# Adding the pooling branch into the merged tile by accumulating DMAs from GpSimd's queue, instead of loading it and adding it on VectorE

## The chip, the cores and the metric

The kernel runs on one core of a Trainium2 chip. The metric is the device time of one execution in microseconds (us): 1882.92 us, the median of three runs (1879.91 to 1883.15).

## What is computed

The reference is one hybrid decoder layer over 512 positions and a model width of 2048, in float32. Cut to the part that the change touches:

```python
merged = sigmoid(gate_pool) * (y_pool @ w_pool_out) + sigmoid(gate_dn) * (y_dn @ w_dn_out)
h = h + merged @ w_o
return rmsnorm(h[:, N_META:], final_norm_w)
```

`y_pool` is 1024 wide, `y_dn` 2048 wide, and `w_dn_out` and `w_o` are 2048 x 2048. Ahead of this come a combined input projection, a pooling mixer and a chunked gated DeltaNet, in which nothing is changed.

## The kernel before

**Layout.** Activations lie transposed: a tile is 128 output channels (partitions) by 512 positions. `merged` has 16 such tiles, k = 0 to 15. Every float32 product is made of three fp32r products: a matrix is split in a high part (a ScalarE copy, `wh`, `xh`, `mh`) and a low part (a VectorE subtraction, `wl`, `xl`, `ml`).

**Stages.** (1) Input projection and both mixers. (2) The pool units: 16 units n, each `y_pool @ w_pool_out` for 128 channels, times its gate (`g0a`, `g0b`, `g0c`), stored by GpSimd's queue in the DRAM scratch `pool_d` (`unit_stored` counts the landings). (3) Eight output blocks for `y_dn @ w_dn_out`, b = DN0 to END - 1, called j = 0 to 7 below; block j makes the tiles `merged[2j]` (c = 0) and `merged[2j+1]` (c = 1). (4) The product with `w_o`: four column blocks, each over the 16 tiles k in order, then residual, norm and store.

**An output block.** It is a Strassen-like product of 2 x 2 quarters with seven products (order 7, 6, 2, 5, 4, 3, NEXT; the last one belongs to the next block, and block 7 has six). Each product is two chunks of 12 matmuls, so a block has 14 chunks, t = 0 to 13 (12 in block 7). Every engine has its own program for a block, written as a loop over t:

- SyncE (`block_loads`) loads the four quarters of the next block's weights into `raw`, 512 KB each. The first load waits for the sum S4 (line 1913) of the block that runs, the second, right behind it, for the eighth low part of a split; the others for later splits. The second load brings the quarter of the product NEXT.
- ScalarE (`block_acts`) makes the high parts (line 1324) some four chunks ahead, snapshots of accumulators, and `last_to_time`, a copy of one accumulator to half of `merged[2j]`.
- VectorE (`block_steps`) makes the low parts (line 1883), the sums of quarters S3, S2, S1, S4 (lines 1891, 1899, 1905, 1913) that the weights of later products need, and the results c22, c21, c11 (lines 1927, 1920, 1934).
- TensorE waits for each chunk for its low part (`lo_done`), then for what the product needs.

The hook `branch(t)` puts the work of the merge into these loops. Before, ScalarE makes `last_to_time` at t = 12 of block j. VectorE multiplies `merged[2j+1]` by its gate `g1` at t = 10, and `merged[2j]` at t = 13 (`weighed_by_gate`, line 2499; each counts up `mg_step`). At t = 5 of the blocks 2 to 5 VectorE adds one tile of the pooling branch (`m_whole`, line 2510), ScalarE makes the high part (`m_split`), and VectorE the low part (`m_low`, line 2515). The tiles 4 to 15 go through the same three steps in the first column block of stage 4, each beside a split of `w_o` (`split_c`, lines 1324 and 2504).

**Where the pooling branch comes from.** SyncE loads `pool_d` back in four pieces of 1 MB (`load_gated`, line 894): the first ahead of block 0's loads, two when the last chunk of block 7 is done, the fourth after the tile multiplications. The gates `g1` are loaded from ScalarE's queue: those of blocks 0 and 1 (`second_gates`, line 1828) behind the last split before block 0 and ahead of block 0's first snapshot, those of block j + 1 at t = 10 of block j, 256 KB x 2 each.

Of the kernel before, what the change touches and what calls it, by code (L numbers as in the profile page):

```python
# [7 lines left out]
ALU = mybir.AluOpType  # L8
# [3 lines left out]
P = 128  # L12
D = 2048
SEQ = 512
# [5 lines left out]
KT = D // P  # L20
# [28 lines left out]
CW = 256  # L49
# [110 lines left out]
def base_of(b):  # L160

    return counted(b, "chunk")
# [76 lines left out]
def build(nc, x, meta_tokens, norm_w, w_in, conv_w, A_log, dt_bias, pool_mix, pool_scale, dn_norm_w,  # L239
# [10 lines left out]
    with outer:  # L250
# [5 lines left out]
        def sem(name):  # L256
            return outer.enter_context(nc.semaphore(name))
# [43 lines left out]
        def layout(number):  # L301
            made = Layout()
            made.stack_id = number
            return made
# [125 lines left out]
        def set_at(product_of):  # L430

            return X_AT + 2 * XA * XPLACE.index(product_of)


        lay = layout(8)
        lay.skip_to(KT * SEQ)
        gated_last = lay.tensor("gated_last", [4, SEQ])
        gated_first = lay.tensor("gated_first", [4, SEQ])
        lay.skip_to(set_at(3))
        gated_set = lay.tensor("gated_set", [2, 4, SEQ])  # L440
        lay.close()
        gated = [gated_first[:, :, :], gated_set[:, 0, :, :], gated_set[:, 1, :, :], gated_last[:, :, :]]


        lay = layout(7)
        xsum = {}
        for product_of in XPLACE:
# [86 lines left out]
        unit_done, unit_stored = sem("unit_done"), sem("unit_stored")  # L534
        yd_loaded = [sem("yd_loaded0"), sem("yd_loaded1")]
        g1_loaded = [sem("g1_loaded0"), sem("g1_loaded1")]
        mg_step, mg_done = sem("mg_step"), sem("mg_done")
        gated_loaded = [sem("gated_loaded0"), sem("gated_loaded1")]

        m_hi, m_lo = sem("m_hi"), sem("m_lo")  # L540
        w_hi, w_lo, w_used, c_done, res_done = sem("w_hi"), sem("w_lo"), sem("w_used"), sem("c_done"), sem("res_done")
# [121 lines left out]

            return (n + 2) % 3

        def m_step(j, t):


            return j - 2 if t == 5 and 2 <= j < 6 else None

        def c0_of(kind):

# [83 lines left out]
        def _(sp):  # L756
# [128 lines left out]
            for units, pieces in ((NUNIT - 2, ((RA, 11), (buffer_of(DN0, DN0 % 2, 7), 21))),  # L885
                                  (NUNIT, ((RF, 22), (buffer_of(DN0, DN0 % 2, 2), 12)))):
                sp.wait_ge(w_lo, 2 * units)
                for slot, quarter in pieces:
                    load_raw(slot, quarter, 0, w_dn_out)

            def load_gated(i):

                rows = pool_d[4 * P * i:4 * P * (i + 1), :].rearrange("(k p) t -> p k t", p=P)
                sp.dma_start(gated[i], rows).then_inc(gated_loaded[i % 2], 16)

            sp.wait_ge(x_lo, SET_LO + 4 * len(SET_SPLITS))
            sp.wait_ge(unit_stored, 16 * NUNIT)
            load_gated(0)
            for b in range(DN0, END - 1):
                block_loads(b, b % 2, (b + 1 - DN0) * CW, None, w_dn_out)  # L900

# [11 lines left out]
            for u in range(4):  # L913
                load_c(u)
            sp.wait_ge(pe_chunk, base_of(END))
            for i in range(1, 3):
                load_gated(i)
            x_rows = x[0].rearrange("(n p) d -> p n d", p=P)
            for i in range(2):
                sp.dma_start(res[:, :, i * 1024:(i + 1) * 1024], x_rows[:, :, i * 1024:(i + 1) * 1024]).then_inc(res_loaded, 16)  # L920
            sp.wait_ge(add_done, counted(END, "add"))
            sp.dma_start(fnw[:, :], final_norm_w.unsqueeze(0).broadcast_to([P, D])).then_inc(fnw_loaded, 16)
            sp.wait_ge(mg_step, KT)
            sp.wait_ge(mg_done, 8)
            load_gated(3)
            for u in range(4, 4 * NCB):
                load_c(u)
            for n in range(4):
# [393 lines left out]
        def _(act):  # L1322
# [71 lines left out]
            def last_to_time(b, par, kind, dst):  # L1394

                act.wait_ge(pe_chunk, last_added(b))
                for part, cols in placed(kind, not eight(b), dst):
                    ins = copy(part, bank_a[par][:, cols])
                ins.then_inc(last_done, 1)
# [415 lines left out]

            def m_split(k):

                act.wait_ge(mg_done, k + 1)
                copy(mhs[k], merged[:, k, :]).then_inc(m_hi, 1)

            def second_gates(j):

                if j > 1:
                    act.wait_ge(mg_step, 2 * j - 2)
                else:
                    act.wait_ge(x_lo, SET_LO + 3 * len(SET_SPLITS))
                for c in range(2):
                    act.dma_start(g1[:, j % 2, c, :], gates_d[D + j * CW + c * P:D + j * CW + (c + 1) * P, :]).then_inc(g1_loaded[j % 2], 16)

            for j in range(2):  # L1830
                second_gates(j)
            for b in range(DN0, END):
                def branch(t, b=b):
                    j = b - DN0
                    if t == 12:
                        last_to_time(b, b % 2, "gate", merged[:, 2 * j, :])
                    if t == 10 and 0 < j < END - 1 - DN0:
                        second_gates(j + 1)
                    if m_step(j, t) is not None:
                        m_split(m_step(j, t))  # L1840
                    if b == END - 1 and t in C_SPLITS:
                        split_c(0, C_SPLITS.index(t))
                block_acts(b, b % 2, "gate", "gate", branch, no_hook)

            last_to_time(END - 1, (END - 1) % 2, "gate", merged[:, KT - 2, :])

            def squares(blk, n):
# [25 lines left out]
        def _(dve):  # L1873
# [629 lines left out]
                dve.wait_ge(w_hi, C_SPLIT + KT * blk + kt + 1)  # L2503
                tt(cwl[kt], rawc[kt // 4][:, kt % 4, :], cwh[kt].bitcast(F32), ALU.subtract).then_inc(w_lo, 1)  # L2504

            def m_whole(k):

                dve.wait_ge(gated_loaded[k // 4 % 2], 16 * (k // 8) + 16)
                dve.wait_ge(mg_step, 2 * (k // 2) + (1 if k % 2 == 1 else 2))
                tt(merged[:, k, :], merged[:, k, :], gated[k // 4][:, k % 4, :], ALU.add).then_inc(mg_done, 1)  # L2510

            def m_low(k):

                dve.wait_ge(m_hi, k + 1)
                tt(ml[:, k, :], merged[:, k, :], mhs[k].bitcast(F32), ALU.subtract).then_inc(m_lo, 1)
# [4 lines left out]
            for b in range(DN0, END):  # L2520
                def branch(t, b=b):
                    j = b - DN0
                    if t == 13:
                        weighed_by_gate(j, 0)
                    if t == 10:
                        weighed_by_gate(j, 1)
                    if m_step(j, t) is not None:
                        m_whole(m_step(j, t))
                        m_low(m_step(j, t))
                    if b == END - 1 and t in C_SPLITS:  # L2530
                        split_c(0, C_SPLITS.index(t))
                block_steps(b, b % 2, "gate", [merged[:, 2 * (b - DN0) + c, :] for c in range(2)], no_wait, branch, no_hook)

            weighed_by_gate(END - 1 - DN0, 0)

            def residual(blk, n):
# [14 lines left out]

            for kt in range(4, KT):
                split_c(0, kt)
                m_whole(kt)
                m_low(kt)
            for blk in range(1, NCB):
                for kt in range(KT):
# [21 lines left out]
        def _(pool):  # L2579
# [89 lines left out]
            def gate_load(n):  # L2669

                pool.dma_start(g0[unit_gate(n)], gates_d[n * P:(n + 1) * P, :]).then_inc(g0_loaded[unit_gate(n)], 16)

            pool.wait_ge(pe_chunk, ALL_CHUNKS)
            pool.wait_ge(add_done, counted(NCP, "add"))
            for c in range(2):
# [3 lines left out]
            for n in range(NUNIT):  # L2679
                pool.wait_ge(unit_done, n + 1)  # L2680
                pool.dma_start(pool_d[n * P:(n + 1) * P, :], g0[unit_gate(n)]).then_inc(unit_stored, 16)
                pool.wait_ge(unit_stored, 16 * n + 16)
                if n + 3 < NUNIT:
                    gate_load(n + 3)
# [1 line left out]
_INS = ["x", "meta_tokens", "norm_w", "w_in", "conv_w", "A_log", "dt_bias", "pool_mix", "pool_scale", "dn_norm_w",  # L2686
        "w_pool_out", "w_dn_out", "w_o", "final_norm_w"]
# [14 lines left out]
```

## Time and profile before

| | |
|---|---|
| median of 3 runs | 1882.92 us |
| the profiled execution, its own time | 1879.91 us |
| its span in the profile | 1877.8 us |
| TensorE matmul busy | 1828.2 us, 97% |
| VectorE, ScalarE, GpSimd busy | 73%, 55%, 6% |
| stage 3, from the first chunk of block 0 | 1536.4 to 1695.8 us |
| stage 4, matmuls | 1695.8 to 1870.0 us |
| mean granted clock of TensorE | 0.996 of full speed |

A timeline row has start, duration, engine, line, operation, output and inputs, and in square brackets the idle time of the engine ahead of it with what ended it. A row with "x2" merges two instructions in a row. DVE is VectorE, ACT ScalarE, PE TensorE, POOL GpSimd, SP SyncE; a "q" behind the name is the engine's sequencer. In the profile's DMA rows q0 is the queue that GpSimd feeds, q1 SyncE's, q10 ScalarE's.

### The profile page before, as it was taken

What the parts mean: (1) busy time and instruction counts of PE and PEld (TensorE: products, weight loads), DVE (VectorE), ACT (ScalarE), POOL (GpSimd) and SP (SyncE); (2) the same over time, 40 slices, a digit from 0 to 9 for tenths busy, and PEclk for the clock granted to TensorE, in tenths of its full rate; (3) what the DMA queues carried; (4) which work ended last, traced back from release to release, by engine and by line L of the source; (5) the groups of instructions that cost most, each with busy time, mean ns of one, the idle gap of its engine ahead of it and who ended that gap; (6) DMA issues with size and microseconds to landing.
All of it is one profiled execution on the core that took longest, in us unless ns stands there. A gap on an engine that the chain in (4) does not pass through costs nothing.

```text
span 1877.8 us, 39178 instructions
## 1 busy us (share of the span) xinstructions
PE 1828.2 (97%) x15889; PEld 1746.1 (93%) x15889; DVE 1378.1 (73%) x2440; ACT 1029.7 (55%) x2299; POOL 120.1 (6%) x156
## 2 busy tenths in 40 slices
PE   7999999999999999999999999999999999999998
PEld 6999999999999999999999998999999889998886
DVE  7777878778787887868788687777785857886442
ACT  6445456566575756757566574645554434444331
POOL 1100000101010010101001010000000110000000
PEclk9999999999999999999999999999999999999999
DMA  6342455555275554536555265455645755467402
GB/s 197 106 127 66 119 163 151 130 148 159 86 199 140 160 130 141 153 110 183 137 146 157 86 189 139 115 167 146 157 119 178 231 184 150 117 190 286 151 23 90
DMA packets 332133, 273.51 MB, mean 146 GB/s; under 512 B 12841, under 2 KB 283650, under 8 KB 331298
## 3 DMA queue, kind: packets, MB, share of 16 engines
q1 hardware_dynamic: 302528, 201.43, 37.9%
q0 software_dynamic: 12992, 39.57, 7.7%
q10 hardware_dynamic: 16434, 30.00, 4.5%
q8 instruction: 126, 2.06, 0.5%
q14 instruction: 53, 0.43, 0.1%
HBM read 225.22 MB, written 46.79 MB: 145 GB/s over the span
## 4 chain that ended last, share of the span: by engine, by line
PE 71%; DMA 9%; DVE 9%; ACT 6%; issue 4%; POOL 1%; ACTq 0%; DVEq 0%; SPq 0%; POOLq 0%
PE pj L1012 43%; PE pj L971 10%; PE pg L939 10%; PE pj L939 5%; PE pt L939 3%; ACT wh L1324 2%; DVE wl L1883 2%; DMA dec<-in_consts 1%; DMA pool_out_scratch<-g0a 1%; DMA pool_out_scratch<-g0b 1%; DVE raw L1913 1%; DMA pool_out_scratch<-g0c 1%; DMA dec<-gate_sum_scratch 1%; PE pt L1144 1%; DVE stg L2227 1%
## 5 line engine op out<-in xcount | busy, mean ns | idle before, releaser
L1012 PE MATMUL pj<-xh,wh 128*128 128x256 f32 (+1 forms) x3016 | 876.4, 291 | 9.4 <-ACT snap L1324 4.5
L1012 PE MATMUL pj<-xl,wh 128*128 128x256 f32 (+1 forms) x3016 | 850.8, 282 | 0.0
L1012 PE MATMUL pj<-xh,wl 128*128 128x256 f32 (+1 forms) x3016 | 850.8, 282 | 0.0
L1324 ACT ACTIVATE wh<-raw 128x512 fp32r<-128x512 f32 x882 | 533.8, 627 | 529.8 <-PE pj L1012 173.3
L1883 DVE TENSOR_TENSOR wl<-raw,wh 128x512 fp32r<-128x512 f32 x854 | 573.8, 689 | 312.4 <-ACT wh L1324 297.3
L1012 PEld LDWEIGHTS pj<-xh,wh 128*128 128x128 f32 x3016 | 569.9, 189 | 19.0 <-ACT snap L1324 6.8
L1012 PEld LDWEIGHTS pj<-xl,wh 128*128 128x128 f32 x3016 | 571.1, 189 | 0.8 <-issue 0.7
L1012 PEld LDWEIGHTS pj<-xh,wl 128*128 128x128 f32 x3016 | 569.8, 189 | 0.0
L971 PE MATMUL pj<-xh,wh 128*128 128x260 f32 (+2 forms) x648 | 185.7, 287 | 3.1 <-DVE wl L1883 3.1
L971 PE MATMUL pj<-xh,wl 128*128 128x260 f32 (+2 forms) x648 | 183.7, 284 | 0.0
L971 PE MATMUL pj<-xl,wh 128*128 128x260 f32 (+2 forms) x648 | 183.4, 283 | 0.0
L971 PEld LDWEIGHTS pj<-xh,wh 128*128 128x128 f32 x648 | 122.7, 189 | 3.6 <-POOL xl L2593 3.4
L971 PEld LDWEIGHTS pj<-xl,wh 128*128 128x128 f32 x648 | 122.9, 190 | 0.2 <-issue 0.2
L971 PEld LDWEIGHTS pj<-xh,wl 128*128 128x128 f32 x648 | 122.5, 189 | 0.0
L2227 DVE SCALAR_TENSOR_TENSOR stg<-xin,convcur,stg 128x528 f32<-128x528 f32 x144 | 109.9, 763 | 8.0 <-ACT stg L1537 7.3
L1324 ACT ACTIVATE snap<-pj 128x256 f32<-128x256 f32 (+2 forms) x182 | 68.7, 378 | 33.4 <-PE pj L1012 21.9
L2504 DVE TENSOR_TENSOR cw_low<-cw_raw,cw_high 128x512 fp32r<-128x512 f32 x64 | 42.6, 689 | 54.6 <-ACT cw_high L1324 54.6
L1899 DVE TENSOR_TENSOR raw<-raw 128x1024 f32<-128x1024 f32 x54 | 66.1, 1224 | 6.3 <-DVE wl L1883 0.5
L1324 ACT ACTIVATE cw_high<-cw_raw 128x512 fp32r<-128x512 f32 x64 | 38.4, 626 | 58.4 <-PE pt L939 29.7
L1905 DVE TENSOR_TENSOR raw<-raw 128x1024 f32<-128x1024 f32 x54 | 65.8, 1219 | 0.0
L1891 DVE TENSOR_TENSOR raw<-raw 128x1024 f32<-128x1024 f32 x54 | 65.8, 1219 | 0.0
L1913 DVE TENSOR_TENSOR raw<-raw 128x1024 f32<-128x1024 f32 x54 | 65.8, 1218 | 0.0
(325 smaller groups left out, 2258.0 us busy)
## 6 DMA issues: line engine op xcount, KB each, us to landing
raw<-in_w_in SPq DMA_DIRECT2D x224, 512.0 KB, 4.7
head_scratch<-stg ACTq DMA_DIRECT2D x64, 264.0 KB, 3.8
raw<-in_w_dn_out SPq DMA_DIRECT2D x32, 512.0 KB, 5.4
cw_raw<-in_w_o SPq DMA_DIRECT2D x16, 1024.0 KB, 6.0
kq<-head_scratch SPq DMA_DIRECT2D x8, 1056.0 KB, 9.7
gates_scratch<-stg ACTq DMA_DIRECT2D x32, 256.0 KB, 2.0
raw<-in_w_pool_out SPq DMA_DIRECT2D x7, 1024.0 KB, 5.9
tm<-head_scratch SPq DMA_DIRECT2D x8, 528.0 KB, 3.6
```

Source lines behind the costliest of these rows:

```text
L939: return pe.matmul(dst, lhs, rhs, start=start, stop=stop)
L971: mm = pe.matmul(banks[bank][:, c0:TH], w[:, slot, k, :], xx[factor][:, kt, c0:TH], start=chunk in opened and one and k == 0, stop=chunk i ...
L1012: mm = pe.matmul(bank[:, c0:TH], w[:, slot, k, :], xx[what][:, kt, c0:TH], start=opens and one and kt == 0, stop=closes and last and kt == ...
L1144: mm = pe.transpose(pt[rows, i * P:(i + 1) * P], src, ident)
L1324: return act.activation(dst, src, ACT.Copy)
L1883: tt(wl[:, slot, :, :], raw[:, buffer_of(of, par, what), HK * half:HK * (half + 1), :], wh[:, slot, :, :].bitcast(F32), ALU.subtract).then ...
L1891: tt(tile, tile, raw[:, RA, :, :], ALU.add).then_inc(sum_done, 1)
L1899: tt(tile, tile, raw[:, RF, :, :], ALU.add).then_inc(sum_done, 1)
L1905: tt(raw[:, buffer_of(b, par, 5), :, :], raw[:, RA, :, :], raw[:, buffer_of(b, par, 6), :, :], ALU.subtract).then_inc(sum_done, 1)
L1913: tt(tile, tile, raw[:, buffer_of(b, par, 2), :, :], ALU.add).then_inc(sum_done, 1)
L2227: dve.scalar_tensor_tensor(acc, xin[:, src_tap:src_tap + T], w, acc, ALU.mult, ALU.add).then_inc(conv_step, 1)
L2504: tt(cwl[kt], rawc[kt // 4][:, kt % 4, :], cwh[kt].bitcast(F32), ALU.subtract).then_inc(w_lo, 1)
```

## The change

The 16 additions `m_whole`, the four loads `load_gated` and their buffers are gone. GpSimd's queue now issues, for each tile, a DMA that reads 256 KB of `pool_d` and adds them to `merged[k]` in place (`accum_op=ALU.add`), once the tile has been multiplied by its gate. The loads of the gates `g1` move from ScalarE's queue to GpSimd's, behind all pool units; those of block j + 2 are issued right behind the accumulation of `merged[2j]`. `last_to_time` and the multiplication of `merged[2j]` move from t = 12 and 13 of block j to t = 0 and 1 of block j + 1. The splits of the tiles 0 to 3 move from t = 5 of blocks 2 to 5 to t = 4 and 6 of blocks 4 and 5. `mg_done` is now counted by the accumulating DMAs, one semaphore for even and one for odd j.

```diff
+        def m_ready(k):
+            return mg_done[k // 2 % 2], 32 * (k // 4 + 1)
...
-            def load_gated(i):
-                rows = pool_d[4 * P * i:4 * P * (i + 1), :].rearrange("(k p) t -> p k t", p=P)
-                sp.dma_start(gated[i], rows).then_inc(gated_loaded[i % 2], 16)
-            sp.wait_ge(x_lo, SET_LO + 4 * len(SET_SPLITS))
-            sp.wait_ge(unit_stored, 16 * NUNIT)
-            load_gated(0)
...
-            for i in range(1, 3):
-                load_gated(i)
...
-            sp.wait_ge(mg_step, KT)
-            sp.wait_ge(mg_done, 8)
-            load_gated(3)
...
             def m_split(k):
-                act.wait_ge(mg_done, k + 1)
+                act.wait_ge(*m_ready(k))
+                if 4 <= k < 12:
+                    act.wait_ge(pe_chunk, base_of(END))
                 copy(mhs[k], merged[:, k, :]).then_inc(m_hi, 1)
-            def second_gates(j):
-                if j > 1:
-                    act.wait_ge(mg_step, 2 * j - 2)
-                else:
-                    act.wait_ge(x_lo, SET_LO + 3 * len(SET_SPLITS))
-                for c in range(2):
-                    act.dma_start(g1[:, j % 2, c, :], gates_d[...]).then_inc(g1_loaded[j % 2], 16)
-            for j in range(2):
-                second_gates(j)
             # ScalarE, branch(t) of block j
-                    if t == 12:
-                        last_to_time(b, b % 2, "gate", merged[:, 2 * j, :])
-                    if t == 10 and 0 < j < END - 1 - DN0:
-                        second_gates(j + 1)
-                    if m_step(j, t) is not None:
-                        m_split(m_step(j, t))
+                    if t == 0 and j > 0:
+                        last_to_time(b - 1, 1 - b % 2, "gate", merged[:, 2 * j - 2, :])
+                    if t in (4, 6) and j in (4, 5):
+                        m_split(2 * (j - 4) + t // 2 - 2)
             # VectorE, branch(t) of block j
-                    if t == 13:
-                        weighed_by_gate(j, 0)
+                    if t == 1 and j > 0:
+                        weighed_by_gate(j - 1, 0)
                     if t == 10:
                         weighed_by_gate(j, 1)
-                    if m_step(j, t) is not None:
-                        m_whole(m_step(j, t))
-                        m_low(m_step(j, t))
+                    if t in (4, 6) and j in (4, 5):
+                        m_low(2 * (j - 4) + t // 2 - 2)
...
             for kt in range(4, KT):
                 split_c(0, kt)
-                m_whole(kt)
                 m_low(kt)
...
             # GpSimd, behind the loop over the pool units
+            pool.wait_ge(x_lo, SET_LO + 3 * len(SET_SPLITS))
+            for j in range(2):
+                second_gates(j)
+            for j in range(D // CW):
+                for step, c in enumerate((1, 0)):
+                    pool.wait_ge(mg_step, 2 * j + step + 1)
+                    if step == 0 and j > 1:
+                        pool.wait_ge(mg_done[j % 2], 32 * (j // 2))
+                    rows = slice(j * CW + c * P, j * CW + (c + 1) * P)
+                    pool.dma_start(merged[:, 2 * j + c, :], pool_d[rows, :], accum_op=ALU.add).then_inc(mg_done[j % 2], 16)
+                if j + 2 < D // CW:
+                    second_gates(j + 2)
```

## Rows read from the trace of the kernel before

**Rows 1.** Windows by stage: us, busy of PE, PEld, DVE, ACT, POOL; clock, DMA share, GB/s.
```profile
1533.90:1540.70 6.80, 5.86 (x28) 5.59 (x27) 4.62 (x6) 1.78 (x3) 1.09 (x2) 0.50 0.33 116
1540.70:1695.90 155.20, 154.72 (x1303) 154.24 (x1303) 127.14 (x188) 73.06 (x146) 0.00 (x0) 1.00 0.53 155
1695.90:1739.50 43.60, 43.60 (x194) 36.09 (x193) 30.80 (x50) 22.08 (x40) 0.00 (x0) 1.00 0.86 319
```

**Rows 2.** The chain that ended last, blocks 3 and 4: start, us, what.
```profile
1606.86 5.43 DMA raw<-in_w_dn_out
...
1626.77 6.48 DMA raw<-in_w_dn_out
```

**Rows 3.** Timeline of VectorE in the blocks 0, 1, 3, 4 and 5.
```profile
1545.43 1.22 DVE L1913 TENSOR_TENSOR raw<-raw 128x1024 f32<-128x1024 f32 x1
...
1565.42 1.22 DVE L1913 TENSOR_TENSOR raw<-raw 128x1024 f32<-128x1024 f32 x1
...
1573.27 1.29 DVE L1883 TENSOR_TENSOR wl<-raw,wh 128x512 fp32r<-128x512 f32 x2 [2.73 <-ACT wh L1324]
...
1605.01 1.22 DVE L1913 TENSOR_TENSOR raw<-raw 128x1024 f32<-128x1024 f32 x1
...
1624.92 1.22 DVE L1913 TENSOR_TENSOR raw<-raw 128x1024 f32<-128x1024 f32 x1
...
1645.28 0.69 DVE L1883 TENSOR_TENSOR wl<-raw,wh 128x512 fp32r<-128x512 f32 x1 [0.16 <-ACT wh L1324]
1645.89 1.22 DVE L1913 TENSOR_TENSOR raw<-raw 128x1024 f32<-128x1024 f32 x1
```

**Rows 4.** Timeline of TensorE, first matmuls of chunks in the blocks 0 to 5, and stage 4's.
```profile
1541.25 0.28 PE L1012 MATMUL pj<-xh,wh 128*128 128x256 f32 x1
...
1550.85 0.29 PE L1012 MATMUL pj<-xh,wh 128*128 128x256 f32 x1
...
1553.69 0.29 PE L1012 MATMUL pj<-xh,wh 128*128 128x256 f32 x1
...
1641.72 0.36 PE L1012 MATMUL pj<-xh,wh 128*128 128x256 f32 x1 [0.34 <-DVE wl L1883]
...
1695.77 0.40 PE L939 MATMUL pg<-cw_high,mh_first 128*128 128x512 f32 x1
```

**Rows 5.** Timeline of VectorE and TensorE in stage 4, tile k = 4.
```profile
1702.98 0.69 DVE L2515 TENSOR_TENSOR ml<-merged,mh 128x512 fp32r<-128x512 f32 x1 [0.70 <-ACT mh L1324]
...
1706.67 0.39 PE L939 MATMUL pg<-cw_high,mh 128*128 128x512 f32 x1
```

**Rows 6.** Timeline of ScalarE, VectorE and GpSimd between the pool units and block 0.
```profile
1538.70 1.88 ACTq L1828 DMA_DIRECT2D g<-gates_scratch  x4
1540.70 0.38 ACT L1324 ACTIVATE snap<-pj 128x256 f32<-128x256 f32 x1 [1.39 <-DMA pool_out_scratch<-g0b]
...
1532.98 0.68 DVE L2442 TENSOR_TENSOR g0a<-g0a,pg 128x512 f32<-128x512 f32 x1
...
1534.21 0.55 POOL L2681 DMA_DIRECT2D pool_out_scratch<-g0a  x1 [4.67 <-DVE g0a L2442]
```

**Rows 7.** Windows of 2 us in block 1, columns as in rows 1.
```profile
1566.00:1568.00 2.00, 2.00 (x19) 2.00 (x19) 2.00 (x4) 1.25 (x3) 0.00 (x0) 1.00 0.08 25
1568.00:1570.00 2.00, 2.00 (x20) 2.00 (x19) 1.73 (x3) 0.63 (x1) 0.00 (x0) 1.00 0.89 251
...
1578.00:1580.00 2.00, 2.00 (x19) 2.00 (x18) 1.59 (x3) 0.51 (x1) 0.00 (x0) 1.00 0.00 0
```

**Rows 8.** DMA, window 1567.2:1567.4: the second load of block 1, us to landing.
```profile
raw<-in_w_dn_out SPq DMA_DIRECT2D x1, 512.0 KB, 5.3
```

**Rows 9.** DMA, windows 1533.9:1537, 1088:1096.1 and 1510.6:1517: packets, MB, share of 16 engines; issues.
```profile
q0 software_dynamic: 80, 0.26, 22.1%
...
pool_out_scratch<-g0a POOLq DMA_DIRECT2D x1, 256.0 KB, 2.3
...
q0 software_dynamic: 192, 0.53, 35.3%
...
q0 software_dynamic: 160, 0.52, 20.6%
...
raw<-in_w_dn_out SPq DMA_DIRECT2D x1, 512.0 KB, 6.6
```

More of the change, by code:

```diff
@@ L432, in set_at @@
             return X_AT + 2 * XA * XPLACE.index(product_of)
[L435 to L442, printed above, removed]
         lay = layout(7)
@@ L536, in build @@
         g1_loaded = [sem("g1_loaded0"), sem("g1_loaded1")]
-        mg_step, mg_done = sem("mg_step"), sem("mg_done")
-        gated_loaded = [sem("gated_loaded0"), sem("gated_loaded1")]
+        mg_step, mg_done = sem("mg_step"), [sem("mg_done0"), sem("mg_done1")]
         m_hi, m_lo = sem("m_hi"), sem("m_lo")
@@ L664, in unit_gate @@
             return (n + 2) % 3
-        def m_step(j, t):
-            return j - 2 if t == 5 and 2 <= j < 6 else None
+        def m_ready(k):
+            return mg_done[k // 2 % 2], 32 * (k // 4 + 1)
         def c0_of(kind):
@@ L1816, in m_split @@
             def m_split(k):
-                act.wait_ge(mg_done, k + 1)
+                act.wait_ge(*m_ready(k))
+                if 4 <= k < 12:
+                    act.wait_ge(pe_chunk, base_of(END))
                 copy(mhs[k], merged[:, k, :]).then_inc(m_hi, 1)
-            def second_gates(j):
-                if j > 1:
-                    act.wait_ge(mg_step, 2 * j - 2)
-                else:
-                    act.wait_ge(x_lo, SET_LO + 3 * len(SET_SPLITS))
-                for c in range(2):
-                    act.dma_start(g1[:, j % 2, c, :], gates_d[D + j * CW + c * P:D + j * CW + (c + 1) * P, :]).then_inc(g1_loaded[j % 2], 16)
-            for j in range(2):
-                second_gates(j)
             for b in range(DN0, END):
@@ L2504, in split_c @@
                 tt(cwl[kt], rawc[kt // 4][:, kt % 4, :], cwh[kt].bitcast(F32), ALU.subtract).then_inc(w_lo, 1)
[L2506 to L2510, printed above, removed]
             def m_low(k):
@@ L2671, in gate_load, with second_gates @@
                 pool.dma_start(g0[unit_gate(n)], gates_d[n * P:(n + 1) * P, :]).then_inc(g0_loaded[unit_gate(n)], 16)
+            def second_gates(j):
+                for c in range(2):
+                    pool.dma_start(g1[:, j % 2, c, :], gates_d[D + j * CW + c * P:D + j * CW + (c + 1) * P, :]).then_inc(g1_loaded[j % 2], 16)
             pool.wait_ge(pe_chunk, ALL_CHUNKS)
```

## The prediction, on record before the run

> **What bounds the kernel now.** I read first the windows by stage. TensorE is busy in 154.7 of the 155.2 us of the eight output blocks, and in all of the 43.6 us of stage 4's first column block [rows 1]. So whatever the change saves on VectorE and ScalarE buys nothing directly; what can move the end is time in which TensorE waits. The next question is how much of that there is in stage 3, and how near the other engines are to making more of it.
>
> TensorE's own timeline answers the first half. From 1550.85 to 1553.69 it starts 24 matmuls, two chunks of 12 [rows 4]: a chunk is 1.42 us, a block of 14 chunks 19.88 us. From the third chunk of block 0 (1541.25) to the third of block 5 (1641.72) lie 70 chunks, 99.4 us, and it took 100.5; from there to stage 4's first matmul (1695.77) lie 38 chunks, 53.96 us, and it took 54.05 [rows 4]. TensorE lost 1.2 us in stage 3. That is all that can be won there.
>
> The second half is in the chain that ended last, where the blocks 3 and 4 pass through the weight loads [rows 2], and in VectorE's timeline. Its sum S4 starts at 1605.01, 1624.92 and 1645.89: periods of 19.91 and 20.97 us [rows 3]. The second load issued behind S4 took 5.43 us in the first and 6.48 us in the second [rows 2]. Take these away and 14.48 and 14.49 us are left. So there is a loop: S4, load, high part on ScalarE, low part on VectorE (VectorE stood idle 2.73 us ahead of it [rows 3]), the sums S3, S2, S1, and S4 of the next block. Its period is 14.48 us plus the landing time l of the second load, and nothing in it waits for TensorE. With l = 5.3 us [rows 8] it is 19.8 us, against TensorE's 19.88. The loop and TensorE run neck and neck, and the loop depends on how fast 1 MB of weights lands.
>
> I measure how late the loop is by the start of S4 minus the start of the block's third chunk. In block 5, where TensorE had just waited for a low part, it is 1645.89 - 1641.72 = 4.17 us; in block 0 it is 1545.43 - 1541.25 = 4.18 us [rows 3, 4]. So 4.17 us is the point from which TensorE waits, and the kernel starts stage 3 on it.
>
> **The change part by part.** *The 16 additions and the loads for them.* Twelve additions lie in stage 4's first column block. Tile 4 is ready at 1702.98 + 0.69 = 1703.7 us and TensorE takes it at 1706.67 [rows 5]: 3 us in hand, so their removal is worth 0. The other four, each with a round trip through ScalarE, stand at t = 5, behind the second load's issue and in VectorE's 2.73 us of idle time: 0 as well. If that cover were gone they would cost about 2 us a block.
>
> *The gate loads off ScalarE's queue.* Ahead of block 0 four issues hold ScalarE's sequencer from 1538.70 for 1.88 us, and the snapshot behind them starts at 1540.70 [rows 6]. The unit store that it waits for, issued at 1534.21, had landed 2.3 us later [rows 9], and the high part ahead of it on ScalarE is done by about 1539.4, so it starts 1.3 us earlier, and with it the splits and sums behind it. The loop enters stage 3 at a lateness of 4.18 - 1.3 = 2.9 us. GpSimd's four issues start only when the last pool unit has landed; block 0 multiplies by its gate only at t = 10, some 13 us behind that, so they are in time.
>
> *`last_to_time` and the multiplication one block on.* The work is the same. On VectorE the multiplication now stands at t = 1 ahead of S4, where it stood at t = 13 ahead of it; it fills the 0.16 us that VectorE waits there [rows 3]. The loop is then 14.32 + l. The last tile loses nothing: block 7 was and is handled behind the loop.
>
> *The accumulations.* That of `merged[2j+1]` follows t = 10, in a stretch where the DMA engines then have nothing to do (share 0.00 [rows 7]): 0. That of `merged[2j]` is issued after the multiplication at t = 1, with the two gate loads of block j + 2 right behind it. All three fall upon the weight loads of the loop, in the blocks 1 to 6. How much extra work is this? A store of 256 KB by this queue took 22.1% of 3.1 us, 0.69 us of all 16 engines; an accumulating load of 512 KB (into `dec`) 35.3% of 8.1 us, so 1.43 us for 256 KB [rows 9]. Together 1.43 + 2 x 0.69 = 2.8 us of DMA work.
>
> How much of it stands in the way? The multiplication ends 1.8 us ahead of the first weight load's issue (a low part and S4 lie between). GpSimd's queue issued its store at 1534.21 after a multiplication that ended at 1533.66 [rows 6], 0.55 us; the store landed 2.3 us later with 0.7 us of work [rows 9], so bytes move about 1.1 us after the issue. The extra traffic therefore begins 0.15 us ahead of the weight load's issue. The weight traffic is at full rate about 1.6 us behind its issue (DMA share 0.08 up to 1568, 0.89 from there [rows 7]). By then 1.75 of the 2.8 us are done, and about 1.1 us are left to share the engines with the second load. Call that delay D. If the accumulation takes longer to issue (0.4 us), D is 1.5; if GpSimd wakes sooner, 0.6. The outer bounds are 0 (all done before) and 2.8 us (all in the way). The nearest row: at 1510 a second weight load ran beside two DMAs of this queue, 20.6% of 6.4 us or 1.3 us of work, and landed in 6.6 us [rows 9] against 5.3 [rows 8], 1.3 us more. I take D = 1.15 us.
>
> On this the Trainium skill (DMA: Bandwidth & Descriptors, section Rules for kernel authors) says that spreading DMAs over issuing engines does not help bandwidth, as all run on the same 16 DMA engines, and that it saves only the sequencer's issue time. The 6.6 us beside 5.3 us agree with it. The same page puts the moving of data at bytes over 436 GB/s; by that the 0.79 MB of extra traffic would be an estimate of 1.8 us instead of 2.8, D would be about 0.1 us, and the sum below would end at its floor of -1.2 us. The trace has durations for the same kind of DMA, so they are used.
>
> **The sum.** The lateness starts at 2.9 us. Block 0's load is free of the extra traffic: 14.32 + 5.3 - 19.88 = -0.26, so 2.64. Six loops follow with l = 5.35 + D, each adding D - 0.21: 2.64 - 1.26 + 6 D = 1.4 + 6 D. TensorE waits for what exceeds 4.17: 6 D - 2.8 us. One second load in seven landed about 1 us late by itself (the 6.48 us); half a chance of that again adds 0.5. Before, TensorE lost 1.2 us. The shift is 6 D - 2.8 + 0.5 - 1.2 = 6 D - 3.5 us, and never below -1.2. With D = 1.15: +3.4 us. With 0.6: +0.1. With 1.5: +5.5. With 2.8: +13.3. The profiled execution's own time is 1879.91 us, its span 1877.8, and 3 us below the median of 1882.92; the same shift on the median gives 1886.3 us.
>
> **Rivals.** *The extra traffic is hidden.* If D is below 0.6 us, the 1.3 us won ahead of block 0 pay for it. For it: the DMA engines are idle just before, and part of the extra traffic fits there. Against: 2.8 us of work have 1.75 us of room. Time: shift -1.2 to 0, 1881.7 to 1882.9, no difference that a measurement of this kernel can tell (it can tell about 0.2%, 3.8 us).
>
> *The accumulation is slower than its rows say, or GpSimd issues it late,* and D is 1.6 to 2.8 us. For it: no accumulation into a tile of this shape is in the trace, and landings of the one into `dec` were 5 us and more. A chain of longer waits could also bring the granted clock down, as it stood at 0.50 for 6.8 us ahead of block 0, after waits of 2 us [rows 1]; that adds up to 3 us, of which the loop would hide most. Time: +6 to +13, 1889 to 1896.
>
> *Faster.* The end would have to come 3.8 us sooner. One mechanism could do it: TensorE lost only 1.2 us in stage 3 [rows 4], so it would have to be the pass from the pool units into block 0, with its half clock for 6.8 us [rows 1]; if the earlier snapshot kept the clock up, some 3 us and the 1.2 would add up to 4. But the clock is down from 1533.9, and the ScalarE issues come only at 1538.7 [rows 6]: it decides only from an effect ahead of its cause. Time: about 1879.
>
> *The tiles come late in stage 4.* Tiles 14 and 15 are accumulated behind 4 MB of other loads. If they landed beyond 1734 us, TensorE would wait; with GpSimd's issue at about 1698 that asks for a landing of 36 us. I give it nothing.
>
> **How the numbers follow.** Hidden: 0.25 (of it 0.22 no difference, 0.03 faster by the spread). The forecast, D from 0.6 to 1.6: 0.5, centred on +3.4 us, which is nearly the 3.8 us that can be told: half of it counts as slower. Slow accumulation: 0.23, slower. Faster: 0.02. So faster 0.05, no difference 0.47, slower 0.48. The range reaches from -1.9 us (the floor and the spread of runs) to +10 (D = 2.3): 1881 to 1893 us.
>
> **What the profile after would show.** The first snapshot of block 0 at about 1539.4 and S4 of block 0 1.3 us earlier; TensorE without a wait in blocks 1 and 2; the second weight load of blocks 1 to 6 landing in about 6.5 us; S4's period at about 20.8 us and TensorE waits of up to 1 us before third chunks from block 3 on; stage 4 still without a wait. I am wrong if the second loads land in under 5.9 us (then nothing is lost), or if a wait that is not in the loop appears: for an accumulation, or for a gate.

## The result, and the profile after

The changed kernel takes 1901.36 us (median of 4 runs, 1898.0 to 1902.85), beside 1881.41 us (4 runs, 1877.3 to 1883.15) for the kernel before: a ratio of 1.0107, 95% interval 1.0084 to 1.0130. It is 20 us slower. The prediction said 1886.3 us, with a range of 1881 to 1893. The sign is right, and the time lies far outside the range. The profiled execution took 1899.81 us.

From the page of the kernel after, the span and the busy time of the engines:

```profile
span 1897.8 us, 39170 instructions
...
PE 1831.1 (96%) x15889; PEld 1747.4 (92%) x15889; DVE 1367.8 (72%) x2424; ACT 1029.0 (54%) x2299; POOL 142.8 (8%) x188
```

TensorE's busy time is 2.9 us longer (1828.2 before), the span 20 us. So most of the time was lost in waiting. The windows by stage of the kernel after, columns as in [rows 1], say in which stage:

```profile
1540.70:1715.80 175.10, 160.54 (x1296) 158.44 (x1295) 124.33 (x184) 72.87 (x144) 21.88 (x31) 0.97 0.61 154
1715.80:1759.40 43.60, 43.60 (x195) 36.09 (x194) 24.89 (x40) 21.60 (x40) 0.84 (x1) 1.00 0.85 302
```

The eight output blocks take 175.1 us instead of 155.2 [rows 1]. Stage 4's first column block takes the same 43.60 us, without a wait: VectorE's busy time there fell from 30.80 to 24.89 us, and bought nothing. The whole 20 us lie in stage 3. What TensorE waits for there is in the waits of the kernel after, window 1540 to 1716 (us in total, times, longest):

```profile
PE pj L987 <- DVE wl L1846: 15.3, 13, 2.8
```

It is the low part of a weight split, 13 times. (The view counts only the idle stretches. The length of the stage gives all that was lost: from block 0's third chunk at 1540.42 to stage 4's first matmul at 1715.82 are 175.4 us, and the 108 chunks between them need 108 x 1.42 = 153.4 us. So TensorE lost 22.0 us; by the same sum it was 1.2 us before. Some 15 us of the 22.0 are idle stretches. The rest is in matmuls that took longer: the first ones behind a wait, and those in three stretches of 3.4 us at half clock. "Wait" below means the whole.) The chain that ended last shows what makes the low part late:

```profile
1566.32 9.00 DMA raw<-in_w_dn_out
1575.40 0.64 ACT wh L1299
1576.06 0.55 DVE wl L1846
1577.28 1.22 DVE raw L1854
1578.93 0.69 DVE merged L2462
1580.96 1.24 DVE raw L1862
1587.97 1.14 DVE raw L1876
1589.73 9.26 DMA raw<-in_w_dn_out
1599.08 0.64 ACT wh L1299
...
1611.64 1.14 DVE raw L1876
1613.41 8.85 DMA raw<-in_w_dn_out
```

This is the loop of the prediction: the second weight load, high part, low part, the sums S3, S2, S1, S4 (line 1876 after), the next load. Its loads take 9.00, 9.26 and 8.85 us, where they took 5.43 and 6.48 us [rows 2]. S4 starts at 1587.97 and 1611.64: a period of 23.67 us, and 23.67 - 9.26 = 14.41 us beside the load, against 14.48 before. The loop is as short as it was, and its load is some 3.6 us longer: over the blocks 1 to 6 the second loads took 9.12 us in the mean (8.54 to 9.69), before 5.54 us (5.26 to 6.48). Six periods of 14.42 + 9.12 us against TensorE's 19.88 make 6 x 3.66 = 22.0 us, the whole wait.

The timeline of the kernel after, from the issue on GpSimd to TensorE's wait:

```profile
1587.67 0.85 POOL L2653 DMA_DIRECT2D merged<-pool_out_scratch  x1 [6.88 <-DVE merged L2462]
1588.22 1.43 POOL L2630 DMA_DIRECT2D g<-gates_scratch  x2
...
1589.18 6.29 SPq L755 DMA_DIRECT2D raw<-in_w_dn_out  x3
...
1599.74 0.69 DVE L1846 TENSOR_TENSOR wl<-raw,wh 128x512 fp32r<-128x512 f32 x1 [6.34 <-ACT wh L1299]
1600.58 0.39 PE L987 MATMUL pj<-xh,wh 128*128 128x256 f32 x1 [2.02 <-DVE wl L1846]
```

GpSimd issues the accumulation 1.5 us and the gate loads 1.0 us ahead of SyncE's first weight load. VectorE, which used to wait 2.73 us for its high part [rows 3], now waits 6.34 us.

How the DMA engines divide their time around these weight loads is in windows of the same block: before the change, with the first weight load issued at 1586.45,

```profile
1585.45:1587.45 2.00, 2.00 (x19) 2.00 (x18) 2.00 (x3) 0.90 (x2) 0.00 (x0) 1.00 0.00 0
1587.45:1589.45 2.00, 2.00 (x19) 2.00 (x18) 1.33 (x3) 0.63 (x2) 0.00 (x0) 1.00 0.78 212
1589.45:1591.45 2.00, 2.00 (x19) 2.00 (x18) 1.97 (x4) 1.05 (x2) 0.00 (x0) 1.00 1.15 313
```

and after it, with that load at 1589.18:

```profile
1588.18:1590.18 2.00, 2.00 (x19) 2.00 (x18) 2.00 (x3) 0.77 (x3) 1.47 (x3) 1.00 0.50 41
1590.18:1592.18 2.00, 2.00 (x19) 2.00 (x19) 1.34 (x4) 1.16 (x2) 0.00 (x0) 1.00 0.80 175
1592.18:1594.18 2.00, 2.00 (x19) 2.00 (x19) 1.10 (x2) 0.00 (x0) 0.00 (x0) 1.00 0.82 228
1594.18:1596.18 2.00, 2.00 (x20) 2.00 (x19) 0.00 (x0) 0.00 (x0) 0.00 (x0) 1.00 1.14 333
```

The last two columns are the DMA share and the GB/s. In the first 5 us behind the issue, 313 GB/s were reached before; after, the engines stand at 175 and 228 GB/s with a share of 0.8. Whose bytes they are is in the DMA view of three stretches after: up to 1.6 us behind the issue (1588.18 to 1590.78), up to 5 us (to 1594.18), and up to 7 us (to 1596.18):

```profile
q0 software_dynamic: 95, 0.19, 62.8%
...
q0 software_dynamic: 267, 0.68, 58.3%
q1 hardware_dynamic: 397, 0.20, 12.5%
...
q0 software_dynamic: 304, 0.79, 46.9%
q1 hardware_dynamic: 1508, 0.77, 34.6%
```

5 us behind the issue the weights (q1) have 0.20 MB. Before they had 1.05 MB there, and after the change they have that much 8.1 us behind it. The weights come about 3 us late in bytes and 3.6 us late in landing.

### The profile page after: what moved, and what is told of

The parts are those of the page before. It is cut to its first block, busy times and chain, and to the rows that moved or that the text cites. A ratio compares the mean times of both kernels' runs of the same rounds, so it can differ in the third digit from the quotient of the medians.

```text
span 1897.8 us, 39170 instructions
## 1 busy us (share of the span) xinstructions
PE 1831.1 (96%) x15889; PEld 1747.4 (92%) x15889; DVE 1367.8 (72%) x2424; ACT 1029.0 (54%) x2299; POOL 142.8 (8%) x188
## 4 chain that ended last, share of the span: by engine, by line
PE 67%; DVE 12%; DMA 10%; ACT 6%; issue 5%; POOL 1%; ACTq 0%; DVEq 0%; SPq 0%; POOLq 0%
PE pj L987 39%; PE pj L946 10%; PE pg L914 10%; PE pj L914 5%; DVE wl L1846 4%; DMA raw<-in_w_dn_out 3%; PE pt L914 3%; ACT wh L1299 2%; DVE raw L1876 2%; DMA pool_out_scratch<-g0b 1%; DMA pool_out_scratch<-g0a 1%; DMA pool_out_scratch<-g0c 1%; PE pt L1119 1%; DVE stg L2190 1%; DVE raw L1854 1%
```

## The experiments

At first three causes stood open: the work of the accumulation is larger than its rows said (W), the adding itself is slow (A), or the gate loads, which the prediction put at 2 x 0.69 us, are the larger part (G). Each experiment below is a single profiled run, except e4 (10 runs) and e8 (12). The edits are against the kernel after and cut to the lines that carry them; helpers, and semaphore counts adapted to them, are left out. l is the mean landing of the second weight load over the blocks 1 to 6, and "wait" is the length of stage 3 from block 0's third chunk, less 153.4 us, as above. The time of a single run says little below some 5 us (runs of the kernel before lie between 1877 and 1888 us), so the readings rest on l and on the wait.

**Accumulation alone (e1).** The gates go back to ScalarE's queue, at t = 10; the accumulations stay.

```diff
 # ScalarE
+            if t == 10 and 0 < j < END - 1 - DN0:
+                second_gates(j + 1)
...
 # GpSimd
-                if j + 2 < D // CW:
-                    second_gates(j + 2)
```

> The changed kernel with one part undone: the gate loads of blocks 2 to 7 go back to ScalarE's queue at t = 10. The accumulation of merged[2j] stays where it is, just ahead of the loop's weight loads. In the changed kernel the second weight load lands in 8.5 to 9.7 us in blocks 1 to 6, against 5.3 to 5.5 before, and the loop's period is 14.41 us plus that. Theory W (work): the DMA engines are shared, and the delay is the work left over; without the gates' 1.4 us of work the load lands 1.4 us sooner than after, in about 7.8 us, time 12 us over before. Theory A (the accumulation blocks): the load still lands in 8.5 us or more, time 16 us or more over before. Theory G (the plain loads behind it on the same queue block): it lands in under 6.3 us, time within 4 us of before.

l = 6.76 us, wait 7.4 us, time 1883.73 us beside 1881.89. So without the gate loads a third of the delay is left: +1.2 us. None of the three forecasts is met: W had 7.8 us, A 8.5 or more, G under 6.3.

**Gates alone (e2).** `merged[2j]` isn't accumulated; the gate loads stay on GpSimd's queue.

```diff
+                    if c == 1:
                     pool.dma_start(merged[:, 2 * j + c, :], pool_d[rows, :], accum_op=ALU.add)...
```

> The changed kernel without the accumulation of the tiles merged[2j] (the even tiles lack the pooling branch; the odd ones have it). The gate loads stay on GpSimd's queue at the same moment. Theory W: 1.4 us of work less, second load in about 7.8 us. Theory A: second load in under 6.3 us, time within 4 us of before. Theory G: 8 us or more, time 12 us or more over before.

l = 6.64 us, wait 6.9 us: +1.1 us, again between the forecasts. The even tiles lack the pooling branch. The time, 1892.8 us, is more than stage 3 explains: block 0's third chunk started at 1548.7 us, 8 us later than in the kernel after. From 1151.2 us TensorE stood at half clock (1.2 GHz) for 23.9 us, where the other runs have 0 to 6.8 us. Only this run's stage 3 is used.

**Plain copies (e3).** Both loads stay, but nothing is added.

```diff
-  pool.dma_start(merged[:, 2 * j + c, :], pool_d[rows, :], accum_op=ALU.add)
+  pool.dma_start(merged[:, 2 * j + c, :], pool_d[rows, :])
```

> The changed kernel with the accumulating DMAs made plain copies of the same bytes from the same queue at the same moments (merged is overwritten by the pooling branch and the y_dn product is lost). Theory W: 0.7 us of work less (0.69 instead of 1.43 for 256 KB), second load in about 8.4 us. Theory A, if it is the adding that blocks: under 6.8 us. Theory G: as after, 8.5 us or more.

l = 7.84 us, wait 14.4 us, 1889.49 us: +2.3 us for the same bytes, against +3.6 with the adding. So of the 3.6 us the adding itself makes 1.3, and the bytes 2.3. (The y_dn product is lost in this kernel; W's 8.4 us is the nearest of the three forecasts.) The DMA work of GpSimd's queue in one block is in the DMA view, in 7 us of e1, 7 us of e2 and 8 us of e3:

```profile
q0 software_dynamic: 144, 0.26, 26.3%
```

```profile
q0 software_dynamic: 160, 0.52, 23.6%
```

```profile
q0 software_dynamic: 240, 0.79, 31.2%
```

The accumulation alone occupies the engines for 0.263 x 7 = 1.84 us (the prediction had 1.43), the two gate loads for 1.65 us (1.38), the plain loads of all three for 2.5 us. In the kernel after it is 0.469 x 8 = 3.75 us for the same 0.79 MB (2.8 in the prediction). The delays of the second load are 1.2, 1.1, 2.3 and 3.6 us: alone, either part hid 0.5 to 0.6 us of its work, and together all but 0.2 us stood in the way. That the accumulation's work isn't blown up by the weights beside it is seen at t = 10, where the same 256 KB move with nothing else under way, in 4 us of the kernel after (1579.92 to 1583.92) and, as a plain copy, in 2.9 us of e3 (1575.35 to 1578.25):

```profile
q0 software_dynamic: 144, 0.26, 43.6%
```

```profile
q0 software_dynamic: 80, 0.26, 25.1%
```

That is 1.74 us for the accumulation (1.5 to 2.2 in the other blocks and runs) and 0.73 us for the copy (0.7 to 1.0).

**The same traffic, late (e4, and e8, the same kernel with more runs).** The accumulation of `merged[2j]` and the gate loads are issued behind the multiplication at t = 10 of block j + 1, where [rows 7] shows the DMA engines idle. Nothing is left out.

```diff
             for j in range(D // CW):
                 pool.wait_ge(mg_step, 2 * j + 1)
+                if j > 0:
+                    accumulate(j - 1, 0)
+                    if j + 1 < D // CW:
+                        second_gates(j + 1)
                 ...
                 accumulate(j, 1)
```

> The whole change with one thing moved: the accumulation of merged[2j] and the gate loads wait for the multiplication at t = 10 of block j + 1, and so fall in the stretch where the DMA engines are idle. All theories that put the loss on the weight loads expect the second load back at 5.3 to 5.9 us, TensorE without waits beyond 1 us in all of blocks 1 to 7, and a time 0 to 2 us under before (the floor of the prediction, -1.2 us). If the time stays 5 us or more over before, the loss is in something else that the change brought (the moved copy and multiplication, GpSimd's queue as such).

> The whole change with accumulation and gate loads moved to t = 10 of the next block, once more and in five rounds, since its difference to before is small: it was 0.11% under before with an interval that touches no change. Expected: 0.05 to 0.15% under before (TensorE's 1.2 us of waits in stage 3 are gone and block 0 starts a little sooner), second loads at 5.3 us.

l = 5.45 and 5.47 us, and TensorE waits for nothing in stage 3: its length is 153.36 us, exactly its chunks. The timeline of GpSimd and the DMA view of 1594 to 1600 in e4:

```profile
1594.90 0.85 POOL L2650 DMA_DIRECT2D merged<-pool_out_scratch  x1 [16.80 <-DVE merged L2462]
1595.45 1.42 POOL L2630 DMA_DIRECT2D g<-gates_scratch  x2
1596.55 1.23 POOL L2650 DMA_DIRECT2D merged<-pool_out_scratch  x1
```

```profile
q0 software_dynamic: 275, 0.71, 56.5%
```

The 0.71 MB of those 6 us move where no weights do. The times are 1879.78 us beside 1881.89 (ratio 0.9989, 0.9977 to 1.0001), and in e8 1878.87 us (12 runs) beside 1880.53 (17 runs): 0.9983, interval 0.9969 to 0.9996. That is 1.7 us faster than before (the interval excludes no change by a hair, and it is under the 0.2% taken as the bound of what can be told), and 22 us faster than the change as made. All of the change's loss is in where the accumulation and the gate loads are issued.

**Another queue (e5, e6).** The prediction held that the issuing engine doesn't matter, as all queues share the same DMA engines. e5 keeps the accumulations and issues the gates from ScalarE at t = 2; e6 does that without the accumulation of `merged[2j]`.

```diff
 # ScalarE
+            if t == 2 and 0 < j < END - 1 - DN0:
+                second_gates(j + 1)
```

> The changed kernel with the gate loads of blocks 2 to 7 issued from ScalarE's queue, but at nearly the moment at which GpSimd issues them in the changed kernel (t = 2, once the multiplication at t = 1 is done). Bytes and moment stay, the queue changes. With the accumulation alone the second weight load landed in 6.8 us on the mean of blocks 1 to 6, with the gates alone in 6.6, with both in 9.1, before in 5.5. Theory W (each extra byte ahead of the weights is served first, whatever queue it is in): about 8 us (the two delays of 1.4 and 1.2 us added), time 12 to 15 us over before. Theory Q (the software queue holds the weights' queue back, and for longer when accumulation and copies follow each other in it): the gates in the other queue cost less, second load under 7.5 us, time under 10 us over before.

> As the run before, and without the accumulation of the tiles merged[2j] (the even tiles lack the pooling branch): 512 KB of gate loads from ScalarE's queue just ahead of the weight loads, nothing on GpSimd's queue there. Theory W: as with the gates alone on GpSimd's queue, second load in about 6.6 us. Theory Q: about 5.8 us, near the 5.5 of before.

e5: l = 7.28 us (Q had under 7.5, W 8), wait 10.5 us, 1887.53 us beside 1880.53. e6: l = 5.50 us (Q 5.8, W 6.6), wait 1.9 us, 1881.3 us. By l the same gate bytes cost 0 from ScalarE and 1.1 us from GpSimd. But ScalarE issued them 1.8 and 1.4 us ahead of the first weight load, GpSimd 1.5 and 1.0, and their first packets ran 0.8 and 0.3 us ahead of it. So queue and moment weren't yet apart.

**The gates from ScalarE, at GpSimd's moment (e9).** As e6, and ScalarE waits for the low part of t = 2 first.

```diff
+                act.wait_ge(lo_done, splits(DN0 + j - 1) + 7)
                 for c in range(2):
                     act.dma_start(g1[...], gates_d[...])
```

> The gate loads alone, from ScalarE's queue as in the run with hardware-queue gates only, but issued 0.6 us later (behind the low part at t = 2), so that their bytes move at the same moment as those of GpSimd's queue did: from about 0.4 us ahead of the first weight load's issue to about 1.3 us behind it. The even tiles lack the pooling branch. With GpSimd's queue the second weight load landed in 6.6 us, with ScalarE's 0.6 us earlier in 5.5. If the moment made that difference, the landing is now 6.3 us or more; if the queue made it, it stays under 5.9 us.

l = 6.12 us, between e6 and e2, which by the expectation decides nothing. Wait 7.0 us, 1886.42 us beside 1879.3. But l is counted from the second load's own issue, and ScalarE, held up here, delays that issue. SyncE's two issues and their landings in e9 (1588.34 and 1589.45), and in e2 (1595.06 and 1595.62):

```profile
raw<-in_w_dn_out SPq DMA_DIRECT2D x1, 512.0 KB, 5.4
...
raw<-in_w_dn_out SPq DMA_DIRECT2D x1, 512.0 KB, 6.2
...
raw<-in_w_dn_out SPq DMA_DIRECT2D x1, 512.0 KB, 5.1
...
raw<-in_w_dn_out SPq DMA_DIRECT2D x1, 512.0 KB, 6.6
```

Over the blocks 1 to 6 the first load took 5.44 us in e9 and 5.28 in e2 (4.13 before), and the second had landed 7.24 and 7.20 us behind the first one's issue (6.09 before, 6.36 in e6). So at the same moment (first gate packets 0.2 and 0.3 us ahead) the gates alone delay the weights equally from either queue: it was the moment, and not the queue as Q had it.

**Earlier by 3.2 us (e7).** `last_to_time` and the multiplication go back to t = 12 and 13, and GpSimd's traffic moves with them.

```diff
-                    if t == 0 and j > 0:
-                        last_to_time(b - 1, 1 - b % 2, "gate", merged[:, 2 * j - 2, :])
+                    if t == 12:
+                        last_to_time(b, b % 2, "gate", merged[:, 2 * j, :])
...
 # VectorE
-                    if t == 1 and j > 0:
-                        weighed_by_gate(j - 1, 0)
+                    if t == 13:
+                        weighed_by_gate(j, 0)
```

> The changed kernel with the copy and the multiplication of merged[2j] put back to t = 12 and 13 of block j; the accumulation and the gate loads stay on GpSimd's queue behind it and so come about 2.4 us sooner against the weight loads. In the changed kernel that traffic ends 5.5 us behind the first weight load's issue. If the second load's delay is the time by which that traffic outlasts the weights' own start (about 1 us behind the issue), it falls from 3.7 us to about 1.4 us: landing in 6.7 us, time 4 to 7 us over before. My forecast's own reckoning (traffic ahead of full rate is free) gives 5.5 us and no loss. If the delay were a fixed cost of having this traffic at all, landing stays near 9 us.

l = 5.90 us, wait 3.3 us, 1883.67 us beside 1880.53. The accumulation is issued 4.7 us ahead of the first weight load instead of 1.5, so 3.2 us sooner and not 2.4 as expected, and GpSimd's last packets run 0.6 to 1.2 us behind that issue instead of 5.3 to 6.6. The same traffic now costs 0.4 us a block instead of 3.6 (5.5 and 6.7 us were the two forecasts of l). So the delay is no fixed price of the traffic: most of it goes when the traffic is nearly over as the weights start. The loop is 14.48 + l here, as before, so the place at t = 1 gave back 0.07 us (the prediction had 0.16).

**The gates first (e10).** Only the order on GpSimd's queue is turned.

```diff
                     if step == 0 and j > 1:
                         pool.wait_ge(mg_done[j % 2], 32 * (j // 2))
+                    if step == 1 and j + 2 < D // CW:
+                        second_gates(j + 2)
                     pool.dma_start(merged[...], pool_d[rows, :], accum_op=ALU.add)...
-                if j + 2 < D // CW:
-                    second_gates(j + 2)
```

> The changed kernel with the order on GpSimd's queue turned round: the two gate loads of block j + 2 first, then the accumulation of merged[2j], the same bytes from the same multiplication on. In the changed kernel the second weight load lands in 9.1 us, with the two delays alone 1.2 and 1.1 us over 5.5. If the surplus (9.1 against 7.8) comes from the gates' copies being interleaved with the weights, it shrinks here, where the copies run ahead of the weights and the accumulation comes last: 8.0 to 8.5 us. If only the sum of the bytes counts, 9.1 us.

l = 8.75 us, wait 19.6 us, 1898.62 us beside 1879.3: +3.2 us instead of +3.6, between the two forecasts (8.0 to 8.5, and 9.1). Within one queue the order is worth 0.4 us at most. Its queue, in 8 us around the loads:

```profile
q0 software_dynamic: 304, 0.79, 40.3%
```

That is 3.2 us of occupation, and the delay is 3.2 us. It is no law: e5 moves the same bytes, the gates first as well, but from ScalarE's queue and 0.5 us sooner, and its delay is 1.7 us.

The landing gives the stage in every run: wait = 6 x (l - 5.5), within 1 us, but for e6 and e9. In these two the second load was issued later behind the first one (0.86 and 1.12 us in the mean, elsewhere 0.56), which l doesn't count; from the first one's issue, 6 x (6.36 - 6.06) = 1.8 and 6 x (7.24 - 6.06) = 7.1 us, they fit too:

| kernel | l, us | 6 x (l - 5.5) | wait, us |
|---|---|---|---|
| before | 5.54 | 0.2 | 1.2 |
| e4, e8 | 5.45, 5.47 | 0 | 0 |
| e6 | 5.50 | 0 | 1.9 |
| e7 | 5.90 | 2.4 | 3.3 |
| e9 | 6.12 | 3.7 | 7.0 |
| e2 | 6.64 | 6.8 | 6.9 |
| e1 | 6.76 | 7.6 | 7.4 |
| e5 | 7.28 | 10.7 | 10.5 |
| e3 | 7.84 | 14.0 | 14.4 |
| e10 | 8.75 | 19.5 | 19.6 |
| after | 9.12 | 21.7 | 22.0 |

## Why the prediction was wrong

**What bounds the kernel: right.** The loop through S4 and the second load, TensorE's chunks beside it, and the threshold between them hold in all eleven kernels of the table.

**The gain ahead of block 0: there, and about as large.** Times from the start of the span can't show it: S4 of block 0 starts at 1545.43 before [rows 3] and 1544.17 after, but in e1 to e10, which differ from the kernel after only behind this point, it lies between 1541.55 (e3) and 1552.47 (e2). Counted from the unit store at 1534.21 before [rows 6] and 1534.46 after, the snapshot stood at 6.49 us and now stands at 5.00, and S4 at 11.22 and now 9.71: 1.5 us, where 1.3 were worked out. (The store that [rows 6] names ahead of the snapshot is `g0b`'s, not the one of 1534.21 that the prediction took. After the change the snapshot starts at 1539.46, before `g0b`'s store of 1538.23 has landed, so it was the four issues that held it, as forecast.) But block 0's third chunk moved too, from 7.04 us behind the store [rows 4] to 5.96, so the lateness started at 3.75 us instead of 2.9. What moved the chunk is the clock, which before stood at half for 6.8 us [rows 1] and in this run of the kernel after didn't:

```profile
1534.00:1540.00 6.00, 4.13 (x33) 3.75 (x32) 4.49 (x6) 2.23 (x5) 1.09 (x2) 1.00 0.22 87
```

In e4 and e8, where it stood at half for 6.8 us again, the chunk is back at 7.04 and 7.00 us and the lateness is 2.67 and 2.72. For the sum it is nearly the same, as TensorE took at once what the loop did not gain. The clock there differs from run to run: of the eleven profiled runs with this code ahead of block 0, six kept it up, three lost it for 3.4 us and two for 6.8.

**The additions, the multiplication, stage 4: right.** The 16 additions were worth nothing, and no tile came late; stage 4's first column block is 43.60 us in both.

**The step that failed** is "By then 1.75 of the 2.8 us are done, and about 1.1 us are left to share the engines with the second load", with "I take D = 1.15 us". D is 3.6 us, beyond even the outer bound of 2.8. Measured from the 5.35 us that the sum had for an undisturbed load, it is 9.12 - 5.35 = 3.77, and 6 D - 3.5 gives +19.1 us; the loop of 14.42 + l instead of 14.32 adds six times 0.1, which makes 19.7 of the 20 us. Two things are wrong in the step:

- The size, 2.8. The traffic occupies the engines for 3.75 us: 1.84 us for the accumulation and 1.65 for the gates when each comes alone (e1, e2), and 0.3 more together. The row of another accumulation [rows 9] was 0.4 us too low for this shape. With the right size and the credit as it was, D would be 3.75 - 1.63 = 2.1 us.
- The credit, 1.75. What runs ahead of the weights' full rate was taken as free. At 1.6 us behind the weight load's issue the engines had indeed spent 0.628 x 2.6 = 1.63 us on GpSimd's queue. But it wasn't free, and the same stretch in e2, e3 and e10 shows it (1.0 us ahead of the issue to 1.6 us behind it: 1594.06 to 1596.66, 1583.61 to 1586.21, 1588.91 to 1591.51):

```profile
q0 software_dynamic: 156, 0.52, 63.5%
...
q0 software_dynamic: 153, 0.53, 62.1%
...
q0 software_dynamic: 142, 0.50, 64.7%
```

In each some 1.65 us are spent, as in the kernel after. In e2 that is the whole of the traffic, nothing is left to share the engines with the weights, and yet they come 1.1 us late. Left at that moment and measured delay are 0 and 1.1 us (e2), 0.2 and 1.2 (e1), 0.9 and 2.3 (e3), 1.5 and 3.2 (e10), 2.1 and 3.6 (after): the delay is 1.0 to 1.7 us more than what is left. So of the 1.63 us at most some 0.6 were free.

Nor are bytes a better measure than occupied time. In the kernel after only 0.19 of 0.79 MB had moved by then, 24%, for 44% of the occupation, and the 0.60 MB left, at the 206 GB/s that all queues together reached from there to 5 us behind the issue (0.70 MB in 3.4 us), would be 2.9 us. But by the same reckoning e10 with 0.29 MB left would be 1.4 us late, and e2 not at all; they were 3.2 and 1.1 us late.

e7 tells the same from the other side: with the traffic 3.2 us earlier, D is 0.4 us.

**The rival "the accumulation is slower than its rows say, or GpSimd issues it late"** named the right side, and half of its cause: the issue wasn't late (1587.67, 0.3 us behind the multiplication's end, where 0.55 were forecast), the accumulation was slower. Its +6 to +13 us stopped at 2.8 us, because I took the sum of the work as the most that can stand in the way. The +1.3 us measured beside a neighbour of 1.3 us of work [rows 9], all of it, was the row that should have set D: it gave no credit for what ran ahead. Scaled to 2.8 us of work it says D = 2.8, +13 us.

**The clock.** The rival named it too. Granted clock was 0.97 of full speed over stage 3. It fell to half (1.2 GHz) for 3.4 us three times, from 1576.9, 1600.8 and 1648.5, each behind a wait of 2.0 to 2.5 us that had ended up to 0.9 us before; behind the longest, 2.8 us up to 1694.7, it did not. As the loop and its loads account for the whole of the 22.0 us, these stretches cost nothing that can be seen: they took the place of waiting.

**The Trainium skill's figure** (DMA: Bandwidth & Descriptors, section Anatomy of one DMA, bytes over 436 GB/s) gave an estimate of 1.8 us for the 0.79 MB, the trace's 3.75 us are twice that, and the sum by that figure, -1.2 us, was further off than mine. Its rule that spreading issues over engines does not help bandwidth (section Rules for kernel authors) agrees with e2 and e9, where the same gates at the same moment delay the weights by the same 1.1 us from either queue. For accumulation and gates together it is open (e5 beside e10).

**What stays open.** Accumulation and gates together delay by 1.3 us more than the two alone (1.2 + 1.1). In the sums that is 0.3 us of occupation and 1.0 us that each part alone hides and both together do not; why not isn't shown. A plain copy alone was not run, so it isn't shown either whether this surplus needs the adding. Why the part that ran ahead was not free in e2, and why e5, with the gates in another queue and 0.5 us sooner than in e10, is late by 1.7 us and not 3.2, is open too: no run has both parts in two queues at e10's moment. What happens in the DMA engines was only seen as the share of 0.8 in the windows.

## What to carry to other kernels

When DMA traffic is moved, look where it falls against the load on the critical loop, and give no credit for what runs in the first microseconds behind that load's issue: here traffic spent by 1.6 us behind it still cost 1.1 us (e2), and traffic issued 3.2 us sooner cost 0.4 (e7). Then look for a stretch of the same period in which the DMA share is 0 and put the issue there: here that turned 20 us of loss into 1.7 us of gain, with the same bytes. Where a loop and the bounding engine run within 0.1 us of each other, multiply every change of the loop's load by the number of its rounds.

## What the runs showed of the hardware

- An accumulating load of 256 KB from DRAM into SBUF occupies the 16 DMA engines for 1.74 us of packet time with nothing beside it and 1.84 us beside weight loads (after, e1), a plain load of the same tile for 0.73 us (e3), or 2.5 - 1.65 = 0.85 us by difference.
- Beside the traffic of GpSimd's queue, issued 1.0 to 1.5 us earlier, a weight load whose own packets are 512 bytes (2075 packets for 1.05 MB) got 0.20 of 0.89 MB in the first 5 us. With 0.52 MB of plain loads in its place, first packets 0.2 to 0.3 us ahead of the weight load's issue, the second weight load landed 1.1 us late from either queue (e2, e9); with first packets 0.8 us ahead, 0.3 us late (e6).
- The share of the DMA engines' time and their progress differ: at a share of 0.50, 2 us moved 0.08 MB when an accumulation started, and at 1.14 they moved 0.67 MB, 0.57 of it weights (1594.18 to 1596.18; a share can be over 1, so packets' times overlap).
